# Matmuls of constants placed in TensorE's idle stretches around each RMS norm of a two-block transformer kernel

## The reference, cut to what matters

```python
def rmsnorm(x, g):
    y = x * lax.rsqrt(jnp.mean(x * x, axis=-1, keepdims=True) + RMS_EPS)
    return y * g

def modulate(z, g, shift, scale):
    return rmsnorm(z, g) * (1.0 + scale) + shift

def swiglu(h, wi, wo):
    a, u = jnp.split(h @ wi, 2, axis=-1)
    return (jax.nn.silu(a) * u) @ wo

# one layer of first_block; mixer_ab in layer 0, pool_mixer in layer 1
x = x + 0.5 * m[2] * swiglu(modulate(x, g0, m[0], m[1]), ffn1_wi, ffn1_wo)
x = x + m[5] * mixer(modulate(x, g1, m[3], m[4]))
x = x + 0.5 * m[8] * swiglu(modulate(x, g2, m[6], m[7]), ffn2_wi, ffn2_wo)
# after the layers: rmsnorm(x, final_g); second_block is one more such layer (hybrid_mixer) and norm
```

## Time and profile before

| | |
|---|---|
| median of 3 runs | 3357.37 us (3356.76 to 3357.43) |
| the profiled execution's own time | 3356.0 us |
| its span (first to last instruction) | 3354.2 us |
| busy share of the span: PE / DVE / ACT / POOL | 93% / 57% / 31% / 1% |
| mean granted clock of TensorE | 0.959 of full speed |
| DMA, mean over the span | 109 GB/s |

### The profile page before, as it was taken

The page is one execution under the profiler, slowest core; times in us unless marked ns, Lnnn a source line. Parts: engine busy times, 40 slices in busy tenths (PEclk is TensorE's granted clock), DMA queues, the critical chain, the costliest instruction groups (busy, mean ns, idle before and its releaser), DMA issues.

```text
span 3354.2 us, 36423 instructions
## 1 busy us (share of the span) xinstructions
PE 3115.9 (93%) x14718; PEld 2500.5 (75%) x14718; DVE 1904.9 (57%) x2720; ACT 1025.3 (31%) x1479; POOL 27.9 (1%) x30
## 2 busy tenths in 40 slices
PE   4999999898889999999997999979998998899998
PEld 3788888786667888778886788768887764577886
DVE  6876555635555544566646555466665655654344
ACT  2322222335443222322224222332223434432222
POOL 2000000000000000000000000000000000000000
PEclk6999999998999999999998999989999999899999
DMA  5434332110023443255532444225551220122321
GB/s 192 132 122 136 126 113 94 55 63 16 1 94 103 160 134 126 81 178 182 189 117 77 157 144 130 96 82 185 198 194 54 76 63 1 51 88 94 101 95 50
DMA packets 101794, 364.98 MB, mean 109 GB/s; under 512 B 11198, under 2 KB 12494, under 8 KB 101372
## 3 DMA queue, kind: packets, MB, share of 16 engines
q1 hardware_dynamic: 97644, 351.65, 31.3%
q10 hardware_dynamic: 2944, 6.29, 0.5%
q0 software_dynamic: 1040, 4.71, 0.4%
HBM read 360.51 MB, written 2.10 MB: 108 GB/s over the span
## 4 chain that ended last, share of the span: by engine, by line
PE 85%; DVE 9%; ACT 3%; issue 1%; DMA 1%; ACTq 0%; POOL 0%; DVEq 0%; SPq 0%
PE ps L197 24%; PE ps L199 24%; PE ps L198 24%; PE ps L201 4%; PE ps L202 2%; DVE WL L189 1%; DVE DUMP L310 1%; DMA STG<-in_w_modt 1%; ACT WH L184 1%; PE ps L513 1%; DVE RAW L1278 1%; PE ps L2323 1%; PE ps L2563 0%; DVE SQ L581 0%; DVE XT L821 0%
## 5 line engine op out<-in xcount | busy, mean ns | idle before, releaser
L197 PE MATMUL ps<-HH,WH 128*128 128x512 f32 x2464 | 980.4, 398 | 35.1 <-DVE HL L570 27.9
L199 PE MATMUL ps<-HH,WL 128*128 128x512 f32 x2464 | 968.5, 393 | 0.0
L198 PE MATMUL ps<-HL,WH 128*128 128x512 f32 x2464 | 968.4, 393 | 0.0
L184 ACT ACTIVATE WH<-RAW 128x1024 fp32r<-128x1024 f32 x456 | 456.9, 1047 | 555.6 <-PE ps L199 410.1
L189 DVE TENSOR_TENSOR WL<-RAW,WH 128x1024 fp32r<-128x1024 f32 x456 | 538.3, 1220 | 86.2 <-ACT WH L184 86.1
L197 PEld LDWEIGHTS ps<-HH,WH 128*128 128x128 f32 x2464 | 468.5, 190 | 143.1 <-issue 40.3
L198 PEld LDWEIGHTS ps<-HL,WH 128*128 128x128 f32 x2464 | 468.6, 190 | 100.4 <-issue 4.6
L199 PEld LDWEIGHTS ps<-HH,WL 128*128 128x128 f32 x2464 | 468.0, 190 | 100.1
L821 DVE SCALAR_TENSOR_TENSOR XT<-ps,DER,XT 128x512 f32<-128x512 f32 x512 | 342.6, 682 | 272.6 <-PE ps L199 258.2
L197 PE MATMUL ps<-GH,WH 128*128 128x512 f32 x1056 | 414.0, 392 | 19.1 <-DVE XT L821 14.3
L762 DVE TENSOR_TENSOR S<-S,ps 128x512 f32<-128x512 f32 x132 | 90.6, 687 | 569.5 <-PE ps L199 569.5
(11 more groups left out here) (355 smaller groups left out, 2410.8 us busy)
## 6 DMA issues: line engine op xcount, KB each, us to landing
RAW<-in_w_modt SPq DMA_DIRECT2D x200, 512.0 KB, 4.5
RAW<-in_ffn_wi SPq DMA_DIRECT2D x176, 512.0 KB, 4.5
RAW<-in_ffn_wo SPq DMA_DIRECT2D x88, 512.0 KB, 4.7
RAW<-in_w_gu SPq DMA_DIRECT2D x88, 512.0 KB, 4.4
RAW<-in_w_in SPq DMA_DIRECT2D x44, 512.0 KB, 3.6
RAW<-in_w_down SPq DMA_DIRECT2D x44, 512.0 KB, 4.6
RAW<-in_w_out SPq DMA_DIRECT2D x16, 512.0 KB, 4.5
MU<-in_w_mod SPq DMA_DIRECT2D x8, 384.0 KB, 8.0
```

The source lines that it names most:

```text
L184: act.e.activation(u.hi, u.ld.view, ACT.Copy).then_inc(u.hi_done.sem, 1)
L197: pe.e.matmul(out, wh, x[0], start=first, stop=False)
L198: pe.e.matmul(out, wh, x[1], start=False, stop=False)
L199: m = pe.e.matmul(out, wl, x[0], start=False, stop=last)
```

## The change

A new step `Busy` emits n float32 products on PE: the identity as weights, 256 columns of constants as the moving operand, into PSUM bank 3. Nobody reads the result, no semaphore is raised, and the only wait it can have is `after`. `rstd_of` adds 4 of them ahead of `RstdSum`, 5 ahead of `RstdSpread`, 5 behind it. In the first block's `final_norm` 2 more follow each of the first seven tiles of `FinalNorm`; the last norm of the kernel has only the 4 ahead of its sum; `mixer_pool` gets 4 more behind its last `PoolMean`, directly ahead of the 4 of the next norm. That is 148 products in all.

```diff
+class Busy(Step):
+    def __init__(self, P, n, after=NONE):
+        self.P, self.n, self.after = P, n, after
+
+    def tensor(self, pe):
+        P = self.P
+        pe.wait_ge(*self.after)
+        for _ in range(self.n):
+            pe.e.matmul(P.banks[3][:, 0:256], P.ID, P.K[:, 0:256], start=True, stop=True)
...
-    def rstd_of(self, nq):
+    def rstd_of(self, nq, ahead=4, last=False):
+        if ahead:
+            self.add(Busy(self, ahead))
         self.add(RstdSum(self, nq))
+        if last:
+            self.add(RstdSpread(self, nq))
+            return
+        self.add(Busy(self, 5))
         self.add(RstdSpread(self, nq))
+        self.add(Busy(self, 5))
...
     def final_norm(self, gname, again):
-        self.rstd_of(T // 128)
-        self.add(FinalNorm(self, gname, Sums(self, T) if again else None))
+        self.rstd_of(T // 128, last=not again)
+        final = self.add(FinalNorm(self, gname, Sums(self, T) if again else None))
+        if again:
+            for k in range(7):
+                self.add(Busy(self, 2, final.done[k]))
...
             mean(3)
+            self.add(Busy(self, 4))
             last = add(3)
```

More of the change, by code:

```diff
@@ L2947, in norm_tiles, with norm_split @@
         return H(sb("HH", [128, 8, T]), sb("HL", [128, 8, T]), sb("HC", [128, 8, 2 * TC]) if two else None)
-    def norm_split(self, ctx, mi, segs, after, ready=False):
+    def norm_split(self, ctx, mi, segs, after, ready=False, ahead=4):
         h = self.norm_tiles(ctx, len(segs) == 2)
         if not ready:
-            self.rstd_of(segs[-1][1] // 128)
+            self.rstd_of(segs[-1][1] // 128, ahead)
         self.add(NormSplit(self, mi, segs, h, after))
```

## The result

The changed kernel takes 3333.95 us (median of 4 runs, 3331.39 to 3334.73), the kernel before 3357.16 beside it (4 runs, 3356.76 to 3357.43): a ratio of 0.9933 (95%: 0.992 to 0.9945), 23 us less. The profiled execution took 3333.18 with a span of 3331.4, so 22.8 less than before by the spans. The mean granted clock rose from 0.959 to 0.976. Lines of the changed file lie 13 further down: the sum is now L502, the spread L526, the low half L583, the square L594; L484 is the new product.

The account below looks back on a forecast made before the run. PE, busy 93% of the span, was taken as the bound. Spreads 8.5, sums 2.8 and first products 11.3, less 0.6 for a late sum, gave 22.0 us: from 3357.4 to 3335.4, range 3329 to 3341.

Parts of the forecast that it names:

- What bounds, and what the gain is: PE's queue bounds the kernel; fillers in the norms' gaps keep TensorE at 2.4 GHz, gaining 22.0 us.
- the rival of the clock that holds in part: About half the norms still lose the clock late; some 11 us are left, 3346; chance 0.12.
- Fit and price: Norm gaps: 0.43 us per filler at full clock; four and five fit, leaving 0.5, 0.5 and 0.4 us.
- Both thin places: End of `mixer_pool`: sum some 0.6 us late; first block's final norm, ahead of feed-forward 6: sum just in time.
- Spreads and sums: At the norms, full clock saves 0.9 us per usual spread, 8.5 together, and 2.8 on four sums.
- The last spread: Last norm of the kernel: only 0.5 us gained, because its gap of 2.63 stays unfilled.
- First products: First 48 matmuls behind each norm take 11.4 us, DVE then being late; 11.3 us gained in all.
- The pool mixer's products wait for DVE anyway: nothing.: First products of the pool mixer: no gain from full clock, as they wait for DVE.
- The 1.6: Forecast gain of the `mixer_ab` stretch, of which 0.7 from first products before PE waits on a weight unit.
- Busy time: PE's busy time over the whole kernel rises by some 60 us (148 x 0.43).
- Given back: DVE, weight loads or mixers' chains take back the 2 to 3 us per stage; 3354; chance 0.08.
- The filler does not count: Clock falls in the second gap despite fillers, which run at half clock; 3.1 us late per norm, 3382; chance 0.07.

Follow-up runs that it names:

- experiment 1: Changed kernel with fillers of 8 columns in place of 256, same number and places: 3354.39 us, ratio 0.9995.
- experiments 2: Changed kernel with each filler as two float32 transposes of 128 columns against the identity: 3344.56 us, ratio 0.9963.
- Experiment 3: Changed kernel without the 5 fillers between sum and spread: 3343.15 us, ratio 0.9965.
- experiment 4: Changed kernel with twice the fillers in `rstd_of` (8, 10 and 10): 3367.01 us, ratio 1.0034.
- experiment 5: Changed kernel with each filler as four float32 transposes of 128 columns against the identity: 3332.55 us, ratio 0.9931.
- experiments 3 and 11: 11 is the changed kernel without the 7 times 2 fillers between the tiles of the first block's final norm: 3331.59 us, one run.
- experiment 7: Changed kernel plus 15 fillers behind the first spread, 5 ahead of the last, 10 ahead of the hybrid mixer's first gated scores: 3331.58 us, ratio 0.9929.

## Why the prediction was right, point by point

**What bounds, and what the gain is.** Right. The sum stood on the clock alone, and experiment 1 shows that of what the fillers bring only the columns that they stream matter; experiments 2 and 3 show that half or two thirds of the filling keep about half of the gain, which is the rival of the clock that holds in part, near its time (3346; they took 3344.56 and 3343.15).

**Fit and price.** Right: 0.43 to 0.45 a product, and idle pieces of 0.51, 0.27 and 0.18 (forecast 0.5, 0.5, 0.4). The two pieces behind the fives are some 0.2 smaller than forecast. Half of that is the first record behind a sum or a spread, which takes 0.32 us to the next start and not 0.22; the rest is in how the records overlap at either end. Both thin places came out: the sum behind the pool mixer is late by 0.69 (forecast 0.6), that of feed-forward 6 is in time.

**Spreads and sums.** Right: 1.15 and 1.04. The last spread was mis-sized. I gave it 0.5 because its gap of 2.63 is open; it took 1.15 nonetheless, and the stretch gave 0.94. Experiment 3 shows the same: once the gap ahead of the sum is filled, the clock often outlasts the next one.

**First products.** Right in size: the five feed-forward stretches came within 0.1 of the forecast, and the 48 matmuls take 11.5 (forecast 11.4). DVE's pace as the next limit holds: it is busy for 11.10 of the 11.40 us of the window, every sixth product starts some 1.45 us after the last one (1387.60, 1389.07, 1390.50), and in experiment 4, where DVE was ahead, the 48 took 11.1.

**The step that failed: "The pool mixer's products wait for DVE anyway: nothing."** The stretch gave 2.18 in place of 0.2: 0.92 for the spread, 1.94 for the products, less 0.69 for the late sum. PE does wait for DVE, for the third pair of low halves, in both kernels, but DVE had waited for PE. The rows of ACT and DVE, first before, then after:

```profile
1775.94 1.03 ACT L1124 ACTIVATE Z<-ps 128x1024 f32<-128x1024 f32 x1 [2.20 <-PE ps L1110]
1776.86 0.62 ACT L989 ACTIVATE WPH<-WP 128x512 fp32r<-128x512 f32 x1
1777.52 0.69 DVE L993 TENSOR_TENSOR WPL<-WP,WPH 128x512 fp32r<-128x512 f32 x1 [2.98 <-ACT WPH L989]
```

```profile
1766.96 1.03 ACT L1137 ACTIVATE Z<-ps 128x1024 f32<-128x1024 f32 x1 [0.25 <-PE ps L1123]
1768.54 0.69 DVE L1006 TENSOR_TENSOR WPL<-WP,WPH 128x512 fp32r<-128x512 f32 x1 [1.04 <-ACT WPH L1002]
```

ACT empties the first group (`Z`) only when PE's half-clock products are done. The next weights (`WPH`) stand behind that in ACT's queue, and DVE's low part of them (`WPL`) waits for ACT, with the next activations behind it in DVE's queue. ACT's wait for PE fell from 2.20 to 0.25 and DVE's for ACT from 2.98 to 1.04, which is the 1.94. Had I followed DVE's wait one step back in the trace of before, it would have been in the sum.

**`mixer_ab`.** The 1.6 came (1.55 by 700 us), and 1.44 went again near 775, where the clock fell for 6.8 us and for 3.4 before. The hybrid mixer lost 0.8 in the same way. In return 1.2 us of the total arose in the first 160 us, long before the first of the added products: the kernel before had a fall of its clock at 96.2 that the changed one had not. These three are the scatter of the clock in stretches that the change does not touch. The sum came out within 1 us because the pool mixer's 2.0 too much, the start's 1.2 and the last norm's 0.4 stand against 2.4 lost in the two mixers. The terms were sound, but that these offset each other is luck.

**Busy time** rose by 43.7, not 60. The fillers' records add 70.2, since each group's last record outlasts the others' step by 0.16, but I had left out that other records become shorter at full clock. One of the three costliest groups, the changed kernel's row:

```profile
L199 PE MATMUL ps<-HH,WL 128*128 128x512 f32 x2464 | 963.2, 391 | 0.0
```

Before, these 2464 had taken 968.5. The three groups of this kind together are 14.8 shorter, the spreads 9.2, the sums 2.8.

**The rivals.** "Given back" did not happen: the lead stays behind each norm, and the 2.4 us lost in the two mixers went where the clock fell in other places. "The filler does not count" is refuted for products by every filled norm and for transposes by experiment 5; its mechanism exists, as experiments 3 and 11 show by five fillers that took 4.63 and 3.95 us where the clock had fallen.

**Left open:** why the clock in the mixers falls in other places from one execution of the same program to the next, and whether experiment 7's late fall follows from its fillers. The best version by its medians is the one without the four extra products (3329.29 and 3331.36, against 3332.37 and 3333.95), but only the 0.69 us at one sum are shown.

## What to carry to other kernels

Where PE is the long queue, look at the granted clock around each chain of short waits, and price what the half clock costs behind the gap, not only in it. Idle PE time can be filled with unread products, if they stream real columns, and if each gap's fill ends before the data does: time it by the gap (here 0.2 to 0.5 us of cover were left), since most of an overrun is paid. When you set a wait to "nothing to gain", follow the releaser one step further: it may itself wait for the engine that becomes faster.

## What the hardware showed that I had not expected

- A float32 transpose of 128 columns leaves one record of 0.11 us, a float32 product of 256 columns two of 0.22, and both held the clock where they filled the same time (experiment 5 and the changed kernel).
- Products of 8 columns look busy in the trace (11.80 of 12.50 us with the rest of the norm) and did not hold the clock (0.50).
- Five executions of the changed kernel lie up to 8.8 us apart (3325.15 to 3333.99). Between two traces of it, 8.0 us apart, 7.5 arose in the mixers, where the clock fell at different places.
